# An encoder layer on one core: a gate column moved ahead, two merges computed in pairs of columns, and a combine without products

## What is computed

```python
h = rmsnorm(x, norm1_w) * (1.0 + sc1) + sh1
y_a, y_b, y_c = o_a @ w_br_a, o_b @ w_br_b, s5_out @ w_br_c         # (1088 x 512) @ (512 x 1024) each
g_a, g_b, g_c = split(sigmoid(h @ w_gate + b_gate), 3)              # (1088 x 1024) @ (1024 x 3072)
x = x + g1 * ((g_a * y_a + g_b * y_b + g_c * y_c) @ w_out)
h = rmsnorm(x, norm2_w) * (1.0 + sc2) + sh2
for e in range(16):                                                 # combine has 2 entries per token
    he = silu(h @ w_exp_gate[e]) * (h @ w_exp_up[e])
    moe = moe + combine[:, e:e + 1] * (he @ w_exp_down[e])
x = x + g2 * moe                                                    # g1, g2: one row for the prompt, one for the sample
y = rmsnorm(x, final_norm_w)
```

## Time and profile before

| | us |
|---|---|
| median of 3 runs (lowest, highest) | 2170.59 (2167.95, 2171.02) |
| profiled execution | 2168.85 |
| its span | 2167.1 |

### The profile page before, as it was taken

How to read it: one execution, slowest core, us unless ns; L and a number is a source line. 1 busy time by engine, 2 the same in 40 slices (tenths; PEclk the granted TensorE clock), 3 DMA queues, 4 the chain that set the end, 5 groups by cost and what they waited for, 6 DMA issues and landing times. The chain is left out here.

```text
span 2167.1 us, 26011 instructions
## 1 busy us (share of the span) xinstructions
PE 1986.4 (92%) x10104; PEld 1266.5 (58%) x10104; DVE 739.8 (34%) x1557; ACT 458.8 (21%) x880; POOL 216.9 (10%) x261
## 2 busy tenths in 40 slices
PE   6999789999989999998889999899999949999976
PEld 3574365654456665655688898766645425555532
DVE  3827712202044111333344444421123343333326
ACT  4220111004123000221212121230001113333322
POOL 2000000000000001210112121010000002322212
PEclk9999989999999999999799999999999969999998
DMA  8085531110020110110000000031320049886217
GB/s 297 32 132 179 201 84 39 43 35 4 0 50 20 30 44 8 32 39 20 21 2 10 11 8 4 26 94 44 106 92 30 39 149 321 295 283 240 90 69 257
DMA packets 144804, 188.36 MB, mean 87 GB/s; under 512 B 21007, under 2 KB 117847, under 8 KB 142599
## 3 DMA queue, kind: packets, MB, share of 16 engines
q1 hardware_dynamic: 126872, 143.07, 21.6%
q0 software_dynamic: 11584, 40.63, 5.5%
q10 hardware_dynamic: 6240, 3.15, 0.5%
HBM read 158.27 MB, written 27.37 MB: 86 GB/s over the span
## 5 line engine op out<-in xcount | busy, mean ns | idle before, releaser
L1464 PE MATMUL cv_ps<-h,late 128*128 128x364 f32 (+1 forms) x576 | 179.1, 473 | 3.1 <-PEq L2865 3.1
L2628 PE MATMUL ex_ps<-ex_ring,ex_xt 128*64 x800 | 178.6, 382 | 2.3 <-DVE ex_xt L2719 2.3
L2629 PE MATMUL ex_ps<-ex_lane_in,ex_xt 128*64 128x256 f32 x800 | 178.6, 382 | 0.0
L1464 PEld LDWEIGHTS cv_ps<-h,late 128*128 128x128 f32 x576 | 110.4, 192 | 71.0 <-issue 7.0
L2628 PEld LDWEIGHTS ex_ps<-ex_ring,ex_xt 128*64 128x64 f32 x800 | 110.4, 138 | 67.7 <-issue 17.7
L2253 PE MATMUL pj_ps<-w_out,mix 128*128 128x512 f32 (+1 forms) x288 | 125.0, 593 | 2.8 <-PEq L2865 2.8
L2068 PE MATMUL go_ps<-h,out_w 128*128 128x364 f32 (+1 forms) x384 | 122.2, 473 | 4.1 <-PEq L2865 4.1
L449 PE MATMUL fr_ps<-h,fr_w_gate 128*128 128x364 f32 (+1 forms) x384 | 121.6, 475 | 1.2 <-DMA fr_w_gate<-in_w_gate 1.2
L1256 PE MATMUL gla_ps<-h,early 128*128 128x364 f32 (+1 forms) x384 | 120.7, 468 | 0.0
L2629 PEld LDWEIGHTS ex_ps<-ex_lane_in,ex_xt 128*64 128x64 f32 x800 | 110.3, 138 | 0.0
L449 PEld LDWEIGHTS fr_ps<-h,fr_w_gate 128*128 128x128 f32 x384 | 72.8, 192 | 51.0 <-issue 8.7
(11 more groups left out here) (506 smaller groups left out, 3003.2 us busy)
## 6 DMA issues: line engine op xcount, KB each, us to landing
fr_y_cols<-in_w_ada SPq DMA_DIRECT2D x8, 2048.0 KB, 7.7
ex_ring<-in_w_exp_gate SPq DMA_DIRECT2D x16, 1024.0 KB, 5.8
ex_ring<-in_w_exp_up SPq DMA_DIRECT2D x16, 1024.0 KB, 9.9
ex_ring<-in_w_exp_down SPq DMA_DIRECT2D x16, 1024.0 KB, 12.5
ys_dram<-ex_y POOLq DMA_DIRECT2D x25, 512.0 KB, 4.3
late<-in_w_in SPq DMA_DIRECT2D x12, 512.0 KB, 4.6
mix<-in_x_prompt SPq DMA_DIRECT2D x8, 512.0 KB, 10.9
glu_w_br<-in_w_ada SPq DMA_DIRECT2D x4, 1024.0 KB, 13.1
```

What stands on the lines that cost most here:

```text
L1464: last = nc.tensor.matmul(ps[n][:, 0:width], g.cv_w(j % 2)[:, k], g.h[:, k, at:at + width], start=k == 0, stop=k == KD - 1)
L2628: nc.tensor.matmul(bank[A, 0:FF], xt[:, s % 2, k, A], own, start=k == 0, stop=k == KD - 1, skip_group_check=True)
L2629: last = nc.tensor.matmul(bank[B, 0:FF], xt[:, s % 2, k, B], lane_in[:, s % 2, k, f], start=k == 0, stop=k == KD - 1, skip_group_check=True)
```

## The change

1. In stage_front EARLY is 7 instead of 6: column 6 of the gates runs before PE's wait for the scan, and ACT makes its sigmoids before it copies the late rows. Column 7 stays behind the rounds.
2. In both merges columns 2 to 7 are computed two columns at a time, in two rounds of 544 tokens each, by a Strassen-Winograd scheme: the gate product of (2 halves of channels) x (2 columns) x (2 quarters of tokens) takes 7 products of half size instead of 8. Each is 4 matmul calls of 272 tokens. DVE makes sums of h once (t1 to t4), sums of the weights for each pair of columns (s1 to s4), and in each round five sums of products; ACT makes a copy and four sigmoids. The branch products stay whole, four of 4 calls a round. The loops are written out, the loads of the raw weights and of the branch weights are separate. In stage_out_merge the sums of h lie where mod_rows and norm_row lay, so SP loads these after the last product, no longer POOL earlier in the stage. g.gla_qk, gla_low and gla_v become parts of one tile.
3. The choice's weight of a row (row_w) is multiplied in `inner`, and the gain g2 into y in the expert stage: DVE writes the gain row of each token (prompt or sample, row_late) into y once the last store has landed, then multiplies the down product in. POOL stores y by an indirect scatter, each row to the place 2 x token + choice of ys_dram (row_home; rows without a token go behind the end). The combine has no stage of its own any more: after the last scatter SP loads both rows of each token, in order, in nine transfers, DVE adds both to x, and the norm follows as before. The gain rows are loaded by SP at the head of the expert stage.
4. stage_route makes row_home, row_w and row_late; the listing holds the number of the choice instead of the token's, and a second listing the weights. `passed` and `owner`, and the two products for the second listing, come ahead of the wait for the first listing's sum.

```diff
@@ stage_front
-        EARLY = 6
+        EARLY = 7
@@ ahead of stage_gla: new
+QW = TOK // 4
+KH = KD // 2
+PRODUCTS = (("x", "a11", "b11", True), ("z2", "s3", "t3", True), ("y", "s2", "t2", True), ("z1", "s1", "t1", True),
+            ("x", "a21", "b21", False), ("z1", "s4", "b22", False), ("z2", "a22", "t4", False))
+OUTPUTS = (("c22", 1, 1), ("c11", 0, 0), ("c12", 0, 1), ("c21", 1, 0))
...
+def pairs_tensor(nc, pe, g, m, group, r):
+    R = ROUNDS_G * (group - 1) + r
+    if r == 0:
+        pe.wait_ge(m.s_step, 4 * group)
+        pe.wait_ge(m.t_step, 4)
+    for name, a, b, start in PRODUCTS:
+        if R and name == "x" and start:
+            pe.wait_ge(m.sig, 4 * R - 2)
+        if R and name == "z2" and start:
+            pe.wait_ge(m.sums, 5 * R)
+        if name == "x" and not start:
+            pe.wait_ge(m.p1_done, R + 1)
+        if name == "z1" and not start:
+            pe.wait_ge(m.sums, 5 * R + 2)
+        if name == "z2" and not start:
+            pe.wait_ge(m.sums, 5 * R + 3)
+        for k in range(KH):
+            last = nc.tensor.matmul(m.bank[name][:, 0:QW], m.weights(group, a, k), m.moving(g, r, b, k), start=start and k == 0, stop=k == KH - 1,
+                                    skip_group_check=True)
+        last.then_inc(m.prod, 1)
+    if r == 0:
+        pe.wait_ge(m.br_loaded, 32 * group)
+    for o, (name, tile, quarter) in enumerate(OUTPUTS):
+        if R:
+            pe.wait_ge(m.mul, 4 * (R - 1) + o + 1)
...
+def pairs_vector(nc, dve, g, m, group, r):
...
+    nc.vector.tensor_tensor(m.v, m.p1, bank["y"], ALU.add).then_inc(m.sums, 1)
...
+    nc.vector.tensor_tensor(c22, m.v, bank["z1"], ALU.add).then_inc(m.sums, 1)
...
+    nc.vector.tensor_tensor(c22, c22, bank["z2"], ALU.add).then_inc(m.sums, 1)
...
+    nc.vector.tensor_tensor(c12, m.v, bank["z1"], ALU.add).then_inc(m.sums, 1)
...
+    nc.vector.tensor_tensor(c21, m.v, bank["z2"], ALU.add).then_inc(m.sums, 1)
+    if r and group < KD // 2 - 1:
+        pairs_sums_of_weights(nc, dve, m, group + 1)
+    for o, (name, tile, quarter) in enumerate(OUTPUTS):
...
+        nc.vector.tensor_tensor(now, now, m.br_banks[o][:, 0:QW], ALU.mult).then_inc(m.mul, 1)
+        dve.wait_ge(m.mul, 4 * R + o + 1)
+        nc.vector.tensor_tensor(mix, mix, now, ALU.add).then_inc(m.add, 1)
@@ stage_gla, tensor (stage_out_merge likewise)
-            with pe.Fori(1, KD // 2) as r:
-                for b in range(2):
-                    column(r * 2 + b, b, r * 32 + 32)
+            pe.wait_ge(merge_gate_done, 6)
+            pe.wait_ge(merge_added, 6)
+            for group in range(1, KD // 2):
+                for r in range(2):
+                    pairs_tensor(nc, pe, g, m, group, r)
@@ stage_gla, vector (stage_out_merge likewise)
-            for j in range(KD):
+            dve.wait_ge(o_psum, NT)
+            pairs_sums_of_h(nc, dve, g, m)
+            dve.wait_ge(gated, NT)
+            pairs_sums_of_weights(nc, dve, m, 1)
+            for j in range(2):
@@ stage_out_merge, sync (the same loads go from gpsimd)
+            sp.wait_ge(m.prod, 14 * (KD // 2 - 1))
+            for j, chunk in enumerate((2, 4, 3)):
+                for who in range(2):
+                    sp.dma_start(g.mod_rows[:, j, who], g.mod_dram[who:who + 1, D * chunk:D * chunk + D].broadcast_to([P, D])).then_inc(g.rows_loaded, 16)
+            sp.dma_start(g.norm_row[:], d["norm2_w"].broadcast_to([P, D])).then_inc(g.rows_loaded, 16)
@@ stage_route, vector
+            for k in range(2):
+                nc.vector.tensor_tensor(tile_w[:, k], tile_w[:, k], wide(g.choice_w[:, k], LIST), ALU.mult).then_inc(S["weights_hot"], 1)
+            then(nc.vector.tensor_tensor(passed[:], ends[:].unsqueeze(1).broadcast_to([P, SUBS, NE]), count.unsqueeze(2).broadcast_to([P, SUBS, NE]), ALU.is_lt))
+            then(nc.vector.tensor_reduce(owner[:], passed[:], AX.X, ALU.add))
             dve.wait_ge(S["summed"], 1)
             nc.vector.tensor_copy(listing[:], ps[2][0:3 * LIST, 0:P]).then_inc(S["listing_out"], 1)
             dve.wait_ge(S["listed"], 1)
-            nc.vector.tensor_copy(g.row_token[:], ps[3][:, 0:SLOTS]).then_inc(S["rows_known"], 1)
+            nc.vector.tensor_scalar(listed[:], ps[3][:, 0:SLOTS], -1.0, 0.0, ALU.add, ALU.max).then_inc(S["number"], 1)
+            dve.wait_ge(S["number"], 1)
+            nc.vector.tensor_copy(listed_i[:], listed[:]).then_inc(S["number"], 1)
+            dve.wait_ge(S["number"], 2)
+            nc.vector.tensor_scalar(g.row_token[:], listed_i[:], 1, None, ALU.logical_shift_right).then_inc(S["rows_known"], 1)
...
@@ stage_experts, sync
+            for who in range(2):
+                sp.dma_start(g.gain[:, who], g.mod_dram[who:who + 1, 5 * D:6 * D].broadcast_to([P, D])).then_inc(g.gains_loaded, 16)
             for e in range(2, NE):
...
+            sp.wait_ge(S["stored"], 16 * SLOTS)
+            for i in range(NT):
+                sp.dma_start(rows[i][0:size(i)], g.ys_dram[2 * P * i:2 * (P * i + size(i)), :].rearrange("(t k) c -> t k c", k=2)).then_inc(rows_in[i], 16)
@@ stage_experts, gpsimd
-                pool.dma_start(g.ys_dram[P * s:P * s + P, :], y[:]).then_inc(S["stored"], 16)
+                nc.gpsimd.indirect_dma_start(g.ys_dram, bass.IndirectOffsetOnAxis(ap=g.row_home[:, s:s + 1], axis=0), y[:], None).then_inc(S["stored"], 16)
@@ stage_experts, vector
-            def store_half(s):
-                dve.wait_ge(S["down_psum"], 2 * s + 2)
+            def gates_of(s):
                 if s:
                     dve.wait_ge(S["stored"], 16 * s)
-                nc.vector.tensor_copy(y[:, 512:], down_ps[1][:]).then_inc(S["y_out"], 1)
+                nc.vector.scalar_tensor_tensor(y[:], gain_diff, g.row_late[:, s:s + 1], g.gain[:, 0], ALU.mult, ALU.add).then_inc(S["y_gain"], 1)
+            def rows_out(s):
+                dve.wait_ge(S["y_gain"], s + 1)
+                for c in range(2):
+                    half = slice(512 * c, 512 * c + 512)
+                    dve.wait_ge(S["down_psum"], 2 * s + c + 1)
+                    nc.vector.tensor_tensor(y[:, half], y[:, half], down_ps[c][:], ALU.mult).then_inc(S["y_out"], 1)
...
             for s in range(SLOTS):
                 if s:
-                    store_half(s - 1)
+                    rows_out(s - 1)
                 if s + 1 < SLOTS:
                     copy_in(s + 1)
...
-                nc.vector.tensor_tensor(inner[:], silu[:], up_ps[:, 0:FF], ALU.mult).then_inc(S["inner"], 1)
+                nc.vector.scalar_tensor_tensor(inner[:], silu[:], g.row_w[:, s:s + 1], up_ps[:, 0:FF], ALU.mult, ALU.mult).then_inc(S["inner"], 1)
...
                 if s + 1 < SLOTS:
                     unload(s + 1)
+                gates_of(s)
+            rows_out(SLOTS - 1)
+            dve.wait_ge(S["final_loaded"], 16)
             for i in range(NT):
                 n = size(i)
+                dve.wait_ge(rows_in[i], 16)
+                nc.vector.tensor_tensor(x1[0:n, i], x1[0:n, i], rows[i][0:n, 0], ALU.add).then_inc(S["half_added"], 1)
+                dve.wait_ge(S["half_added"], i + 1)
+                nc.vector.tensor_tensor(x1[0:n, i], x1[0:n, i], rows[i][0:n, 1], ALU.add).then_inc(S["added"], 1)
                 if i:
                     finish(i - 1)
             finish(NT - 1)
```

More of the change, by code:

```diff
@@ L885, in _, with __init__, weights, moving @@
             mix(2)
+QW = TOK // 4
[3 more added lines that the diff above has]
+OUTPUTS = (("c22", 1, 1), ("c11", 0, 0), ("c12", 0, 1), ("c21", 1, 0))
+ROUNDS_G = 2
+class Pairs:
+    def __init__(self, sem, banks, br_banks, raw, w_br, t, s, p1, v, sets):
+        self.prod, self.p1_done, self.sums, self.sig, self.br, self.mul, self.add, self.t_step, self.s_step, self.br_loaded = (sem(f"pair_{n}") for n in (
+            "prod p1_done sums sig br mul add t_step s_step br_loaded").split())
+        self.raw_loaded = [sem(f"pair_raw_loaded{b}") for b in range(2)]
+        self.bank = dict(zip(("x", "y", "z1", "z2"), banks))
+        self.br_banks, self.raw, self.w_br, self.t, self.s, self.p1, self.v, self.sets = br_banks, raw, w_br, t, s, p1, v, sets
+    def weights(self, group, name, k):
+        if name[0] == "s":
+            return self.s[int(name[1]) - 1][:, k]
+        return self.raw[group % 2][int(name[2]) - 1][:, KH * (int(name[1]) - 1) + k]
+    def moving(self, g, r, name, k):
+        if name[0] == "t":
+            return self.t[int(name[1]) - 1][:, k, r]
+        at = 2 * QW * r + QW * (int(name[2]) - 1)
+        return g.h[:, KH * (int(name[1]) - 1) + k, at:at + QW]
+    def out(self, R, name):
+        return self.sets[R % 2][("c22", "c11", "c12", "c21").index(name)]
@@ new lines, in pairs_tensor @@
+def pairs_tensor(nc, pe, g, m, group, r):
[23 more added lines that the diff above has]
+            pe.wait_ge(m.mul, 4 * (R - 1) + o + 1)
+        at = 2 * QW * r + QW * quarter
+        for k in range(KB):
```

(32 more changed lines are left out.)

340 lines of the change are left out of this document (200 added, 140 removed).

## The result

| | before | after |
|---|---|---|
| median of 4 runs, us (lowest, highest) | 2169.55 (2167.95, 2171.02) | 2134.11 (2129.77, 2136.81) |
| profiled execution: span, us | 2167.1 | 2131.3 |

A forecast was written before the change was run, and what follows sets the result against it. TensorE, busy 92% of the span, was taken as the bound. Front -11.0, merges -19.4, route +1.4, gains +3.3 and tail -16.4 sum to -42.1 from 2168.85, so 2127 us; range 2116 to 2143.

The forecast's parts named there:

- Merges: GLA merge and stage_out_merge: columns 2 to 7 in pairs need fewer MATMUL rows, -9.7 us each, -19.4 together.
- rival A: Both merges: DVE or ACT answer late and PE waits in each of 12 rounds, 1 us a round, 2139; chance 0.13.
- z1 slack: Inside a merge round: DVE is done at 8.0 us, PE wants the reused bank z1 at 9.2; no loss taken.
- Row vectors on SP's queue: stage_out_merge: mod_rows and norm_row land some 4.4 us behind PE's end, hidden with some 3 us of slack; 0.
- Route: stage_route: added DVE operations ahead of the listing's copy (+1.0) and from listing to row_token (+0.4), +1.4 us.
- Front: stage_front: column 6 runs in PE's wait for the scan; S5's end stores are late next; -11.0 us.
- Gains: Head of the expert stage: 1 MB of gain loads ahead of expert 2 delays its third matrix in slot 0, +3.3 us.
- Slots: Expert slots of 12.3 us, all PE's: the added DVE work and the scatter are hidden, 0.
- Rival C: Expert slots: a scatter landing above 9.6 us lengthens each slot; at 12.3 us landing, 2192 us; chance 0.09.
- Tail: From the last row store's issue to the end: 66.6 us become 50.2, set by the DMA, -16.4 us.
- The sum by DVE: Tail: scatter landing, first MB, nine times two additions and a scaling, then the end: 47.8 us, against 50.2 by DMA.
- Rival B: Tail: the DMA stays at today's 231 GB/s and bounds it, 65.5 us, total 2142; chance 0.11.

The follow-up runs named there:

- gains_late: The changed kernel with the two gain loads moved behind expert 2's three matrices on SP's queue, DVE waiting just ahead of slot 0's gain row: 2127.37 us, 0.9801.

## Why the prediction was right, and where not

- **Merges**: -9.7 each forecast, -9.8 and -9.9 in the traces, -9.8 alone. The price of a 272-column MATMUL from stage_glu held, 0.23; rival A did not come: the z1 slack of 1.2 us was enough, no wait shows inside a round, and DVE's sums ahead of column 0 were hidden.
- **Row vectors on SP's queue**: DVE waited for them until 1574.45, 6.6 us behind the merge's end instead of the 4.4 of the sum, and the first product still found them. Hidden, as forecast.
- **Route**: +1.4 forecast, and +1.30 in the piece that it priced, up to the first gather. That the whole line also reads +1.3 is luck: the slow start of stage_project and the shorter way from gather to stage, neither of them in the sum, cancel.
- **Front**: the mechanism held, and S5's end stores were late next; -11.0 became -10.1, because the rounds began 1.15 later. ACT's late copies were level with the scan, as the sum had it (282.01 and 281.82); the scan itself ended 0.87 later in this execution. From the rounds on, the gain is 11.3. The failed step is the one after: the sum ended at the start of stage_glu and let the clock be. In the rows before, stage_glu began behind 1.77 us of standing; the change makes it 5.23, and that stood in the sum's own numbers (column 7 ends at 314.6, the next stage at 320.1) without being priced. The clock gave 4.1 back.
- **Gains**: the mechanism was right, the size wrong: +3.3, and +6.8 measured. The price of a megabyte was taken from matrices; at the head of the stage the gain rows, one row spread over 128 partitions, went at 171 to 199 GB/s. Since gains_late shows no such slow stretch for the same rows, the term that was mis-sized is that of a load at the head of the queue; why it is slow there stays open. The 2.25 in slot 1, at a clock of 0.50 behind PE's stand, were not in the sum.
- **Slots**: the 0.06 of `inner` lies on PE's path. The idle 3.40 ahead of that operation was read as slack; but DVE waits there for PE, and PE then for DVE, so a longer operation costs its difference in each slot. The scatter's issue beside DVE's copy took 1.4 more (2.36 against 0.96), close to the 1.5 that was expected. Rival C was read too strictly: L reached 10.8, above 9.6, and nothing was lost, because DVE's wait for it (3.61 at most, in the last of three late slots in a row) took time in which DVE would have been idle.
- **Tail**: -16.4 forecast, -20.7 measured. Of the two chains the wrong one was put last. The price of 3.35 us a MB from three matrices in a row held no more: with nothing else running the DMA moved 424 GB/s, 2.5 us a MB. The sum by DVE, 47.8, was near the 45.9; the scatter's landing was 3.3 rather than 5.0, and the first megabyte came 4.9 us after its issue rather than 5.8. Rival B is far off. (The lower bound of the gain, 0.8, is 1.1 by rival B's own 65.5.)

The errors of +6.2 in slot 0, the clock behind it and `inner`, +4.1 in the clock behind the front and +0.9 in the front outweigh the -4.3 in the tail and the small ones; so the span's change is 6.3 short of the forecast, the median is 7 above it, and the time is inside the range. That it came so near is partly luck, because errors of both signs met.

## What to carry to other kernels

A gain ahead of a stage boundary is not finished at the boundary: look at how long TensorE will then stand there, and at what clock the next stage starts. A duration that two engines hand to and fro in every iteration has no slack, even where the trace shows idle time just before it. And look at what a new transfer stands ahead of: the same gain rows cost TensorE a stand of 6.78 us at the head of the queue, ahead of the matrix that it waits for, and one of 2.30 behind it.
